# Projections, merges and MLP products of a hybrid encoder layer as plain float32 matmuls in place of three matmuls of split halves

## What is computed

```
u = RMSNorm(x) * norm1
p = u @ w_in                      # 1024 -> 7696 columns: three mixers' inputs and merge gates
o_A = neighbourhood attention     # reads its columns of p
o_B = bidirectional gated DeltaNet
o_C = bidirectional RG-LRU, times gelu(gate)
merged = sum_b sigmoid(G_b) * (o_b @ w_br[b])     # three branches, 512 -> 1024
x = x + merged @ w_out                            # 1024 -> 1024
v = RMSNorm(x) * norm2
x = x + relu(v @ w_mlp1)^2 @ w_mlp2               # 1024 -> 4096 -> 1024
y = RMSNorm(x) * norm_f
```

## Time and profile before

| | |
|---|---|
| runs of the kernel before, us | 3174.47, 3175.49, 3176.71; median 3175.49 |
| profiled execution, first to last instruction (span) | 3173.1 us |
| TensorE matmuls (PE) busy | 3016.9 us, 95% |
| TensorE weight loads (PEld) busy | 2465.5 us, 78% |
| VectorE (DVE) busy | 1325.8 us, 42% |
| ScalarE (ACT) busy | 1106.9 us, 35% |
| GpSimd (POOL) busy | 1141.1 us, 36% |
| HBM traffic | 113 GB/s over the span |

### The profile page before, as it was taken

How to read it: one execution, slowest core, us unless ns; L and a number is a source line. 1 busy time by engine, 2 the same in 40 slices (tenths; PEclk the granted TensorE clock), 3 DMA queues, 4 the chain that set the end, 5 groups by cost and what they waited for, 6 DMA issues and landing times. The chain is left out here.

```text
span 3173.1 us, 44125 instructions
## 1 busy us (share of the span) xinstructions
PE 3016.9 (95%) x17907; PEld 2465.5 (78%) x17907; DVE 1325.8 (42%) x1933; ACT 1106.9 (35%) x1859; POOL 1141.1 (36%) x754
## 2 busy tenths in 40 slices
PE   5999999999999978799997999979999999999998
PEld 4778787888887745688886787868888888888887
DVE  4233232311379868677764244122223223332323
ACT  4131312132134357666663212232333333232322
POOL 4211121112111020232110342456666666666764
PEclk8999999999999989899998999989999999999999
DMA  3534232333545265210100644333333333323331
GB/s 96 171 137 131 74 115 82 126 100 113 167 145 173 106 229 162 100 52 22 72 20 19 225 157 148 125 123 93 93 107 89 97 93 120 106 87 100 95 120 65
DMA packets 239417, 353.14 MB, mean 111 GB/s; under 512 B 32752, under 2 KB 186096, under 8 KB 239216
## 3 DMA queue, kind: packets, MB, share of 16 engines
q1 hardware_dynamic: 239216, 350.32, 34.0%
HBM read 263.71 MB, written 96.36 MB: 113 GB/s over the span
## 5 line engine op out<-in xcount | busy, mean ns | idle before, releaser
L102 PE MATMUL pj_acc<-u_hi,pj_w_hi 128*128 128x512 f32 x1464 | 589.9, 403 | 14.9 <-POOL u_lo L531 13.0
L2353 DVE TENSOR_TENSOR x_tm<-m_ps,x_tm 128x512 f32<-128x512 f32 x384 | 265.0, 691 | 744.8 <-PE m_ps L104 744.8
L104 PE MATMUL pj_acc<-u_hi,pj_w_lo 128*128 128x512 f32 x1464 | 571.9, 391 | 0.0
L103 PE MATMUL pj_acc<-u_lo,pj_w_hi 128*128 128x512 f32 x1464 | 571.4, 390 | 0.0
L524 POOL TENSOR_TENSOR pj_w_lo<-pj_w_raw,pj_w_hi 128x1024 fp32r<-128x1024 f32 x61 | 150.2, 2463 | 840.5 <-ACT pj_w_hi L559 840.5
L102 PEld LDWEIGHTS pj_acc<-u_hi,pj_w_hi 128*128 128x128 f32 x1464 | 275.8, 188 | 81.4 <-POOL u_lo L531 13.9
L2230 POOL TENSOR_TENSOR m_w_lo<-m_w_raw,m_w_hi 128x1024 fp32r<-128x1024 f32 x96 | 237.8, 2499 | 263.0 <-ACT m_w_hi L2144 263.0
L103 PEld LDWEIGHTS pj_acc<-u_lo,pj_w_hi 128*128 128x128 f32 x1464 | 276.0, 189 | 65.3 <-issue 9.6
L104 PEld LDWEIGHTS pj_acc<-u_hi,pj_w_lo 128*128 128x128 f32 x1464 | 275.6, 188 | 58.4
L102 PE MATMUL m_ps<-m_v_hi,m_w_hi 128*128 128x512 f32 x768 | 299.9, 390 | 2.4 <-DVE m_v_lo L2321 2.4
L103 PE MATMUL m_ps<-m_v_lo,m_w_hi 128*128 128x512 f32 x768 | 299.7, 390 | 0.0
(11 more groups left out here) (259 smaller groups left out, 5215.6 us busy)
## 6 DMA issues: line engine op xcount, KB each, us to landing
m_w_raw<-in_w_mlp_dram SPq DMA_DIRECT2D x48, 1024.0 KB, 5.5
m_w_raw<-in_w_mlp_dram SPq DMA_DIRECT2D x96, 512.0 KB, 3.7
proj<-pj_stage SPq DMA_DIRECT2D x61, 768.0 KB, 3.5
pj_w_raw<-in_w_in_dram SPq DMA_DIRECT2D x61, 512.0 KB, 4.9
mo_gate<-proj SPq DMA_DIRECT2D x24, 768.0 KB, 4.4
mo_w_raw<-in_w_out_dram SPq DMA_DIRECT2D x48, 256.0 KB, 2.6
rpb_bias<-pj_shut SPq DMA_DIRECT2D x48, 192.0 KB, 3.0
rpb_bias<-rpb_near SPq DMA_DIRECT2D x24, 384.0 KB
```

The source lines that it names most:

```text
L102: pe.matmul(out, w_hi, x_hi, start=first, stop=False)
L103: pe.matmul(out, w_hi, x_lo, start=False, stop=False)
L104: return pe.matmul(out, w_lo, x_hi, start=False, stop=last)
L2353: dve.tensor_tensor(xt, ps2[:, q % 4], xt, ALU.add).then_inc(added, 1)
```

## The change

All `mm3` calls become one `pe.matmul` on float32 operands. The casts and the subtractions go from ACT, POOL and DVE, with their buffers and semaphores. Weights land where TensorE reads them, with more buffers: 4 in `front` (`wt`), 6 in `merge_project`, 3 for each of the two MLP weights. SP's loads wait for TensorE's own semaphores (`mm_done`, `slot_done`, `up_done`, `part_done`). In `front` DVE writes the turned tile times the gain directly into `u`. In `merge_project` branch inputs are loaded directly into `under_x` and `held`, with one semaphore for each branch and token block (four pieces), the loads of the gates stand between those of the first branch's pieces, and the factor 0.5 moves from `m_hi`/`m_lo` to the addition to `x_tm`. In `mlp` the second weights come in one load of 1024 KB a group, POOL writes the square directly into `h`, and ACT copies the turned tile into `v`. Nothing is changed in `attention` and `deltanet`.

```diff
-def mm3(pe, out, w_hi, w_lo, x_hi, x_lo, first, last):
-
-    pe.matmul(out, w_hi, x_hi, start=first, stop=False)
-    pe.matmul(out, w_hi, x_lo, start=False, stop=False)
-    return pe.matmul(out, w_lo, x_hi, start=False, stop=last)
...
             def load_w(n):
-                if n >= 2:
-                    sp.wait_ge(lo_done, n - 1)
+                if n >= NW:
+                    sp.wait_ge(mm_done, n - NW + 1)
                 c = column(tiles[n])
-                sp.dma_start(w_raw[:, n % 2], w_t[:, :, c:c + P]).then_inc(w_in[n % 2], 16)
+                sp.dma_start(wt[:, n % NW], w_t[:, :, c:c + P]).then_inc(w_in[n % NW], 16)
...
-            def low_w(n):
-                pool.wait_ge(hi_done, n + 1)
-                pool.tensor_tensor(w_lo[:, n % 2], w_raw[:, n % 2], w_hi[:, n % 2].bitcast(F32), ALU.subtract).then_inc(lo_done, 1)
...
-            def high_w(n):
-                act.wait_ge(w_in[n % 2], n // 2 * 16 + 16)
-                if n >= 2:
-                    act.wait_ge(mm_done, n - 1)
-                act.copy(w_hi[:, n % 2], w_raw[:, n % 2]).then_inc(hi_done, 1)
...
-                return mm3(pe, acc[:, b * NTB + tb], w_hi[:, b, k], w_lo[:, b, k], u_hi[:, k, sl], u_lo[:, k, sl],
-                           k == 0, k == KD - 1)
+                return pe.matmul(acc[:, b * NTB + tb], wt[:, n % NW, k], u[:, k, sl], start=k == 0, stop=k == KD - 1)
...
-                    dve.tensor_tensor(uf[:, j % 2, k], turn[:, half], gcol[:, k].unsqueeze(2).to_broadcast([P, KD // 2, P]),
+                    dve.tensor_tensor(u[:, k, j * P:(j + 1) * P], turn[:, half], gcol[:, k].unsqueeze(2).to_broadcast([P, KD // 2, P]),
                                       ALU.mult).then_inc(scaled, 1)
...
             load_w(0)
-            for q in range(KB):
-                load_o(q)
+            load_o(0, 0)
             load_w(1)
-            for q in range(KB, PIECES):
-                load_o(q)
             load_gate(0)
+            load_o(0, 1)
             load_gate(1)
+            load_o(0, 2)
...
                         for k in range(KB):
-                            if sl == 0:
-                                pe.wait_ge(o_first, tb * KB + k + 1)
-                            w = slice(k * P, (k + 1) * P)
-                            last = mm3(pe, acc(sl)[:, tb], w_hi[:, b, w], w_lo[:, b, w], o_half(br, k, o, 0), o_half(br, k, o, 1),
-                                       k == 0, k == KB - 1)
+                            last = pe.matmul(acc(sl)[:, tb], wt[:, b, k * P:(k + 1) * P], branch_in(br, k, o), start=k == 0, stop=k == KB - 1)
...
-                    last = mm3(pe, out(t), m_hi[:, c, m], m_lo[:, c, m], w_hi[:, b], w_lo[:, b], c == 0, c == KD - 1)
+                    last = pe.matmul(out(t), total[:, c, m], wt[:, b], start=c == 0, stop=c == KD - 1)
...
-                    dve.tensor_tensor(xt, out(t), xt, ALU.add).then_inc(added, 1)
+                    dve.scalar_tensor_tensor(xt, out(t), 0.5, xt, ALU.mult, ALU.add).then_inc(added, 1)
...
             def load_w1(gg):
-                if gg:
-                    sp.wait_ge(w1_lo_done, 2 * gg)
+                if gg >= NW:
+                    sp.wait_ge(up_done, 2 * (gg - NW + 1))
...
                     pool.wait_ge(relu_done, m + 1)
-                    pool.tensor_tensor(rel[:, j], rel[:, j], rel[:, j], ALU.mult).then_inc(sq_done, 1)
-                    pool.wait_ge(hh_done, m + 1)
-                    pool.tensor_tensor(h_lo[:, m % 4], rel[:, j], h_hi[:, m % 4].bitcast(F32), ALU.subtract).then_inc(hl_done, 1)
+                    if gg >= 2:
+                        pool.wait_ge(part_done, NQ * (gg - 1))
+                    pool.tensor_tensor(h[:, m % 4], rel[:, j], rel[:, j], ALU.mult).then_inc(sq_done, 1)
...
-                        last = mm3(pe, ps1[:, j], w1_hi[:, m % 4, k], w1_lo[:, m % 4, k], v_hi[:, k], v_lo[:, k],
-                                   k == 0, k == KD - 1)
+                        last = pe.matmul(ps1[:, j], w1t[:, gg % NW, k, j * P:(j + 1) * P], v[:, k], start=k == 0, stop=k == KD - 1)
```

More of the change, by code:

```diff
@@ L15 @@
 F32 = mybir.dt.float32
-F32R = mybir.dt.float32r
 U8 = mybir.dt.uint8
@@ L81, in sb @@
         return self.ctx.enter_context(self.nc.sbuf_tensor(f"{self.name}_{name}", [P] + list(shape), dt))
[L83 to L87, removed]
     def ps(self, name, shape):
@@ L234, in conv_steps, with front @@
         c.wait()
-def front(nc, sources, gain, w, proj, o_t, conv_w, conv_b, w_r, b_r, w_i, b_i, lam, u_hi, u_lo, ident, ones, rpb, v_mid, near,
+def front(nc, sources, gain, w, proj, o_t, conv_w, conv_b, w_r, b_r, w_i, b_i, lam, u, ident, ones, rpb, v_mid, near,
           bias_t, g_rows, cols, a_log, dt_bias, dn_w, dn_y):
@@ L287, in front @@
     with Space(nc, "pj") as s:
-        w_raw = s.sb("w_raw", [2, KD, P])
-        w_hi, w_lo = s.sb("w_hi", [2, KD, P], F32R), s.sb("w_lo", [2, KD, P], F32R)
+        wt = s.sb("wt", [NW, KD, P])
         stage = s.sb("stage", [2, T])
@@ L454, in _ @@
                     load_w(1)
+            for n in range(2, NW):
+                load_w(n)
             sp.dma_start(cb[:], conv_b.rearrange("(i p) -> p i", p=P), allow_slow_non_contiguous=True).then_inc(param_in, 16)
@@ L527, in _ @@
             pool.memset(eps[:], EPS).then_inc(eps_made, 1)
[L528 to L535, removed]
+            pool.wait_ge(scaled, 2 * NT)
             conv_zero(pool, xpad, zeroed)
             for p in range(1, NSL):
-                if p + 1 < NSL:
-                    low_w(p + 1)
                 i = lru(p, 1)
@@ L1813, in merge_project, with branch_in @@
     PIECES = KB * NTB
+    NW = 6
     with Space(nc, "mo") as s:
[L1816 to L1820, removed]
+        held = s.sb("held", [KB, T])
+        total = s.sb("total", [KD, T])
+        wt = s.sb("wt", [NW, TB])
         gate = s.sb("gate", [3, T])
         ps = s.ps("ps", [8, TB])
-        w_in = [s.sem(f"w_in{b}") for b in range(3)]
-        o_in = [s.sem(f"o_in{b}") for b in range(4)]
+        w_in = [s.sem(f"w_in{b}") for b in range(NW)]
+        o_in = [[s.sem(f"o_in{br}{tb}") for tb in range(NTB)] for br in range(NB)]
         g_in = [s.sem(f"g_in{b}") for b in range(3)]
         x_in = [s.sem(f"x_in{b}") for b in range(NT)]
-        (w_hi_done, w_lo_done, o_hi_done, o_first, o_lo_done, g_prod, gated, slot_done, mh_done, ml_done, out_done,
-         added) = (s.sem(x) for x in ("w_hi_done", "w_lo_done", "o_hi_done", "o_first", "o_lo_done", "g_prod",
-                                      "gated", "slot_done", "mh_done", "ml_done", "out_done", "added"))
+        g_prod, gated, slot_done, out_done, added = (s.sem(x) for x in ("g_prod", "gated", "slot_done", "out_done", "added"))
         block = s.block()
         w_t = w_br.rearrange("b (k p) n -> p b k n", p=P)
-        m_hi = held
-        def o_half(br, k, sl, low):
+        def branch_in(br, k, sl):
             o = under_x if br % 2 == 0 else held
[L1837 to L1848, removed]
+            return o[:, k, sl]
         def acc(q):
@@ L1921, in _ @@
                     sp.dma_start(x_tm[:, t], rows[t]).then_inc(x_in[t], 16)
[L1923 to L1934, removed]
-                    act.wait_ge(slot_done, KD)
-                act.copy(o_half(br, k, sl, 0), stage[:, q % 4]).then_inc(o_hi_done, 1)
-            def high_m(c):
-                act.wait_ge(gated, MS - KD + c + 1)
-                act.wait_ge(slot_done, 2 * KD)
-                act.activation(m_hi[:, c], total[:, c], ACT.Copy, scale=0.5).then_inc(mh_done, 1)
-            high_w(0)
-            for q in range(PIECES):
-                high_o(q)
-            for sl in range(SLOTS):
-                br, c, rd = at(sl)
-                if sl + 1 < SLOTS:
-                    high_w(sl + 1)
-                if br is not None:
-                    if br == NB - 1 and c:
-                        high_m(c - 1)
-                    for q in pieces_at(br, c):
-                        high_o(q)
-                elif sl == MS:
-                    high_m(KD - 1)
-        @block.gpsimd
-        def _(pool):
-            def low_w(sl):
-                pool.wait_ge(w_hi_done, sl + 1)
-                pool.tensor_tensor(w_lo[:, sl % 2], w_raw[:, sl % 3], w_hi[:, sl % 2].bitcast(F32), ALU.subtract).then_inc(w_lo_done, 1)
-            def low_o(q):
-                br, k, sl = piece(q)
-                pool.wait_ge(o_hi_done, q + 1)
-                pool.tensor_tensor(o_half(br, k, sl, 1), stage[:, q % 4], o_half(br, k, sl, 0).bitcast(F32), ALU.subtract).then_inc(o_lo_done, 1)
-            low_w(0)
-            for sl in range(SLOTS):
-                br, c, rd = at(sl)
-                if sl + 1 < SLOTS:
-                    low_w(sl + 1)
-                if br is not None:
-                    for q in pieces_at(br, c):
-                        low_o(q)
         @block.tensor
@@ L2014, in _ @@
         def _(dve):
-            for q in range(PIECES):
-                br, k, sl = piece(q)
```

(29 more changed lines are left out.)

191 lines of the change are left out of this document (67 added, 124 removed).

## The result

The changed kernel takes 3754.8 us (median; 3752.8 to 3755.6) against 3176.1 before: ratio 1.182, 95% interval 1.1805 to 1.1839. The forecast was 3775, 20 us too much. The page of its profiled execution gives a span of 3753.9 us.

The account below looks back on a forecast made before the run. TensorE, busy 95% of the span, bounds the kernel: 3480 dearer products add 621.9 us to 3173.1 and 22 come back, so span 3773 and median 3775 us, range 3740 to 3806.

Parts of the forecast that it names:

- The bound and the price: Full TensorE bounds front, merges and MLP; 3480 products go from 0.680 to 0.8587 us each, +621.9 us.
- Rivals 3 and 4: 3: one record per call, product 0.429 us, about 2300 us, 1%; 4: chained passes cost 0.2267 each, 3942 us, 4%.
- the Trainium skill's rule: Warm matmuls of N columns follow after N/2.4 + 2.5 ns; with four float32 passes, some +751 us, not used in the sum.
- Rivals 1 and 2: 1: late loads in the merge stage, 3823 us, 3%; 2: clock falls under plain float32 work, 3925 us, 3%.
- the three signs against me: Spacing other than 0.429, TensorE waits for DMA in the merge stage, or clock under 0.97 over front or MLP.
- What comes back: Waits ended by removing casts and subtractions in front, merges and MLP start: 22 us back, bounds 5 to 33.
- Front, start: Before the first projection product, u_hi and u_lo go (3.5 us) and DVE is freer: 5 us gained, bounds 3 to 7.
- the two later waits for u_lo: Front's later time blocks: 6 us gained of 8.5 waited, plus 3 for the clock no longer falling after them.
- Front, small waits put at nothing: Elsewhere in front and MLP TensorE waits 3.2 us in 2086; counted as no gain.
- MLP, start: Without w_hi and v_lo casts ahead, the first MLP product comes near 2103 for 2108.68: 5.5 us gained, bounds 3 to 7.
- Merges: One w_lo wait of 2.8 us, followed by a 0.66 clock, goes: 4.5 us gained, net 2.5 after the start's charge.
- the 2 that I charged for their first loads: At the merges' start the first product waits for all four pieces, with gate tiles between: 2 us lost, bounds 0 to 8.

Follow-up runs that it names:

- e1_price: The kernel before, each `mm3` made one plain float32 matmul on the hi halves, all casts, subtractions and waits kept; 3786.9 us, ratio 1.1919.
- e2_three: The changed kernel, each product made three float32r records on one fixed pair of tiles, still no casts; 3141.7 us, ratio 0.9886.
- e7_order: The kernel before, split halves kept, only orders changed in the front's first slices, the merges' end and the MLP's start; 3163.1 us, ratio 0.9956.
- e8_two: The kernel before without the third record of `mm3` (w_lo by x_hi), all casts and subtractions kept; 2559.1 us, ratio 0.8056.

## Why the prediction was right, and where it was not

**The bound and the price: right.** The count of 3480 and two records a call hold; 0.8584 us a product was measured for 0.8587, so +620.8 for +621.9. Rivals 3 and 4 are out with it: records in chains of 16 (MLP first product) cost what the four of L714 cost. Of the Trainium skill's rule ("TensorE: Matmul & The Clock Gate", "Back-to-back issue gap"; +751, an estimate): its 2.5 ns beyond the columns is what a plain record shows here (429.1 - 426.7), but once for two passes, and the split-half record has 13 ns; the measurement decides.

**Rivals 1 and 2: did not come.** Of the three signs against me, one came in the letter: in the merges TensorE waits 15.1 us for DMA, 3 times. But 13.8 of it is the wait for the stage's first inputs, which was 12.67 before too, for DVE's half of the same piece; the two others are 0.4 and 0.9 us for later pieces of the first slot, and no wait for weights or gates follows. In the front and the MLP TensorE waits for no DMA, and the clock is 1.00 over both long stages.

**What comes back: the term that was mis-sized, 40 for 22.** It is all of the miss but 2 us, and it lies outside its own bounds of 5 to 33; the whole forecast kept its range because the price, a term fifteen times as large, was off by 1.1. Most places were named, and most were too small.
- *Front, start, 8.2 for 5.* I let `xn` start where it had. ACT's cast of the first weights (13.53 to 14.57) stood ahead of its table load and the root; without it `xn` starts at 14.36 for 16.12. And a DVE instruction that reads only SBUF is held up beside POOL's subtraction: of the twelve `xn` before, the five that overlap one last 1.43 to 2.86 us, the seven others 0.741 to 0.745; in e1_price, which keeps the subtractions, the longest is 2.83. Duration of `xn` (ns min/median/max) before:

```profile
L781 DVE TENSOR_SCALAR pj_xn<-pj_x,pj_rstd x12: 741/745/2856, 16.1 to 61.9; 128x1024 f32<-128x1024 f32 x12
```

  and after:

```profile
L740 DVE TENSOR_SCALAR pj_xn<-pj_x,pj_rstd x12: 744/746/754, 14.4 to 51.2; 128x1024 f32<-128x1024 f32 x12
```

- *The clock, left out at two starts.* I charged its fall after the two later waits for u_lo, but not that the first products of the front and of the MLP ran at the lower level. From 24 to 80 us the granted clock was 0.85 before:

```profile
24.00:80.00 56.00, 41.87 (x193) 34.00 (x194) 31.34 (x60) 18.78 (x27) 29.25 (x15) 0.85 0.17 15
```

  and is 1.00 after:

```profile
24.00:80.00 56.00, 54.43 (x175) 27.06 (x174) 24.47 (x55) 5.98 (x11) 0.16 (x3) 1.00 0.36 75
```

  In the front the products before ran three times some 3.2 us at the lower level. A record takes 0.4263 there for 0.2267, so 47% of that time is lost: 4.6 (an estimate), for the 3 I gave back. In the MLP it is 4.9 us (2108.7 to 2113.6), 2.3 lost, over half of its 4.2.
- *Front, small waits put at nothing.* 1.9 us for w_lo, and some 2 for the float32r records behind turns and gates, whose spacing is longer than 0.2267 (last section). With 6.9 of u_lo's waits (8.5 less the 1.6 that are left for `u`) and the 4.6 this makes 15.4 of the 16.2.
- *MLP, start, 7.6 for 5.5.* Two turns ran at the lower clock in my sum (1.97 us); the last took 1.09, as the clock had risen before it.
- *Merges, 5.9 for 4.5.* The 2.2 lost in the stretch before them looks like the 2 that I charged for their first loads, but is not that: e1_price has the loads as they were, and this stretch takes 635.7 us there, 635.6 in the changed kernel. The wait itself grew by 1.1 (12.67 to 13.8). So the agreement is luck, and where the rest of the 2.2 comes from stays open.

e1_price splits the 40 by the spans: 5 from longer products, 35 from the missing casts (32 by the medians); e2_three finds 35 (38) at three records. e7_order shows by experiment that 13 of them are a few waits; the rest is placed by stretch and read from the traces, not tested one by one.

**Slips that changed nothing.** In the earlier trace rows no line but the three of `mm3` is over 0%, where I wrote 1%. The parts of the return add up to 6.5 to 30.4, not 5 to 33, and the lower end to 3745, not 3743. The 3902 of rival 4 leaves out the 2.4 us outside the span.

## What to carry to other kernels

Where TensorE is full, cost a change of number format by passes over the columns: find a matmul of the new kind in the same trace, count its records per call, and take the spacing of a run, not a duration. Casts beside a full TensorE are worth only the few places where they end a wait, mostly at the starts of stages, here 1% in all, but count there the clock and the engine they share with others too. When products get shorter, the same casts can come to bound (the MLP of e8_two), so price both together.

## What the runs showed of the hardware

- A plain float32 matmul of 512 columns is two records of 429.1 ns, a float32r one is one of 226.7; with 256 columns 215.8 and 120. Beyond the passes that is 2.5 and 13 ns a record, at both widths.
- DVE's TENSOR_SCALAR and SCALAR_TENSOR_TENSOR on SBUF alone took up to 2.86 us for 0.745 and up to 3.45 for 1.28 while POOL subtracted (five of five overlapping and three of five), and never over 0.754 and 1.286 with those subtractions gone; its TENSOR_TENSOR from PSUM stayed at 0.69 in both.
- For about ten records after a plain matmul or a turn the float32r spacing is mostly 230 to 236 ns, in the kernel before and on the fixed tiles of e2_three alike; plain records show nothing of the kind (429.2 from the second on).
